# A block-causal attention mask added by TensorE: each masking matmul moved behind its own score map and cut from 64 contraction rows to one

## The reference, cut to what matters

```python
def attend(qb, qpb):
    s = jnp.einsum('bqhmd,bkhmd->bhmqk', qb, k).astype(jnp.float32) * scale
    mask = k_chunk[None, :] <= (qpb // CHUNK)[:, None]
    s = jnp.where(mask[None, None, None], s, -jnp.inf)
    p = jax.nn.softmax(s, axis=-1)
    pd = p[:, :, 0] - lam * p[:, :, 1]
    return jnp.einsum('bhqk,bkhv->bqhv', pd.astype(v.dtype), v)
```

## Time and profile before

| | us |
|---|---|
| median of 3 runs | 755.13 |
| lowest, highest | 754.0, 755.38 |
| the profiled execution | 755.38 |
| its span in the profile | 753.6 |
| PE (TensorE matmul) busy | 680.4 (90%) |
| DVE busy | 521.6 (69%) |
| ACT busy | 423.2 (56%) |
| mean granted TensorE clock | 0.959 |

### The profile page before, as it was taken

How to read it: one execution, slowest core, us unless ns; L and a number is a source line. 1 busy time by engine, 2 the same in 40 slices (tenths; PEclk the granted TensorE clock), 3 DMA queues, 4 the chain that set the end, 5 groups by cost and what they waited for, 6 DMA issues and landing times.

```text
span 753.6 us, 9418 instructions
## 1 busy us (share of the span) xinstructions
PE 680.4 (90%) x3464; PEld 548.7 (73%) x3464; DVE 521.6 (69%) x695; ACT 423.2 (56%) x600; POOL 139.3 (18%) x161
## 2 busy tenths in 40 slices
PE   5999999998879998889999389999999999999960
PEld 4898887776657666678888278888888888888850
DVE  4436745566566674466466868899999999988943
ACT  6645642345544443443333348778888877888750
POOL 4102930010000110100001302222222122222232
PEclk9999999999998999999999579999999999999976
DMA  8634143222580000230084869999999999999562
GB/s 312 200 114 157 54 160 142 65 82 107 204 339 10 2 1 1 62 134 1 1 310 168 337 243 352 368 381 374 381 373 379 376 375 385 374 382 374 187 239 76
DMA packets 33012, 161.63 MB, mean 214 GB/s; under 512 B 6238, under 2 KB 6572, under 8 KB 18253
## 3 DMA queue, kind: packets, MB, share of 16 engines
q1 hardware_dynamic: 23392, 140.39, 48.8%
q0 software_dynamic: 5488, 10.66, 5.2%
q10 hardware_dynamic: 4092, 10.08, 3.6%
HBM read 149.59 MB, written 20.55 MB: 226 GB/s over the span
## 4 chain that ended last, share of the span: by engine, by line
PE 70%; DVE 14%; DMA 7%; ACT 3%; issue 3%; POOL 1%; SPq 1%; POOLq 0%; ACTq 0%; DVEq 0%
PE pj L2098 40%; PE scores L2098 12%; PE tr_v L2098 10%; DVE wl L1407 3%; PE tr_a L2106 2%; PE scores L2475 2%; PE tr_v L2106 2%; DMA acc_rows<-y,idx_sb 1%; PE tr_a L2498 1%; DVE w_lo L1436 1%; DMA xT_raw<-in_xT 1%; DVE tiny L1658 1%; DVE w_lo L1407 1%; ACT prob L1127 1%; DVE hid L1407 1%
## 5 line engine op out<-in xcount | busy, mean ns | idle before, releaser
L1407 DVE TENSOR_TENSOR wl<-moe_raw,wh 128x2048 fp32r<-128x2048 f32 x96 | 218.5, 2290 | 32.0 <-ACT wh L899 31.5
L899 ACT ACTIVATE wh<-moe_raw 128x2048 fp32r<-128x2048 f32 x96 | 182.3, 1919 | 37.4 <-PE scores L2098 12.3
L2098 PE MATMUL pj<-w_hi,xT_hi 128*128 128x512 f32 (+2 forms) x192 | 70.7, 368 | 9.0 <-DVE w_lo L1436 8.3
L739 POOL TENSOR_SCALAR rs<-stat 128x1 f32<-128x1 f32 (+4 forms) x31 | 8.0, 258 | 339.4 <-ACT sq_scr L911 178.7
L2098 PE MATMUL pj<-w_hi,xT_lo 128*128 128x512 f32 (+2 forms) x192 | 68.9, 359 | 0.0
L2098 PE MATMUL pj<-w_lo,xT_hi 128*128 128x512 f32 (+2 forms) x192 | 68.9, 359 | 0.0
L794 POOL DMA_INDIRECT acc_rows<-y,idx_sb x14 | 22.2, 1589 | 207.0 <-ACT y L1329 193.0
L2098 PE MATMUL pj<-wh,xgh 128*128 128x512 f32 x128 | 52.5, 410 | 1.4 <-DVE xgl L1407 1.4
L2098 PE MATMUL scores<-wh,hTh 128*128 128x512 f32 x128 | 51.0, 398 | 1.4 <-DVE hTl L1407 1.4
L1436 DVE SCALAR_TENSOR_TENSOR w_lo<-raw,pack_a,w_hi 128x512 fp32r<-128x512 f32 (+2 forms) x64 | 43.8, 745 | 11.5 <-ACT w_hi L943 11.4
L2098 PE MATMUL tr_v<-wh,xgh 128*128 128x512 f32 x128 | 51.2, 400 | 0.0
(11 more groups left out here) (409 smaller groups left out, 1490.1 us busy)
## 6 DMA issues: line engine op xcount, KB each, us to landing
moe_raw<-in_w_exp_gate SPq DMA_DIRECT2D x32, 1024.0 KB, 7.9
moe_raw<-in_w_exp_up SPq DMA_DIRECT2D x32, 1024.0 KB, 9.1
moe_raw<-in_w_exp_down SPq DMA_DIRECT2D x32, 1024.0 KB, 8.9
raw<-in_dense SPq DMA_DIRECT2D x16, 1024.0 KB, 6.0
raw<-in_dense SPq DMA_DIRECT2D x8, 256.0 KB, 6.2
x_rows<-in_x_prompt SPq DMA_DIRECT2D x4, 512.0 KB, 11.2
xw<-in_x_prompt ACTq DMA_DIRECT2D x1, 2048.0 KB, 8.3
h_rows<-h ACTq DMA_DIRECT2D x4, 512.0 KB, 3.8
```

What stands on the lines that cost most here:

```text
L739: link(pool.tensor_scalar(rs[rows, n, cs], stat[rows, n, cs], EPS, None, ALU.add))
L899: act.activation(wh[s4][:, :], moe_raw[n % RING][:, :], ACT.Copy).then_inc(hi_done, 1)
L1407: return dve.tensor_tensor(out, a, b, op)
L2098: return pe.matmul(out, lhsT, rhs, start=start, stop=stop, skip_group_check=True)
```

## The change

The constants shrink to 65 partitions, with ones on all of them in the first 64 columns of `hide_q`. The mask of a map now takes a single partition of them, 0 for map 0 and 64 for map 1, so that it contracts over one row: 1 x -1e30. And it is issued right behind its own map's scores, ahead of the other map's. The increment of `sc_full` stays on the last mask.

```diff
-        hide_q = put("hide_q", [P, P], BF16)
-        hide_k = put("hide_k", [P, CH], BF16)
+        hide_q = put("hide_q", [CH + 1, P], BF16)
+        hide_k = put("hide_k", [CH + 1, CH], BF16)
...
             link(pool.memset(hide_q[:, :], 0.0))
-            for m in range(2):
-                link(pool.memset(hide_q[DH * m:DH * m + 1, 0:CH], 1.0))
+            link(pool.memset(hide_q[:, 0:CH], 1.0))
             ready(pool.memset(hide_k[:, :], -1e30))
...
                         out = half(key)[:, 512 * m:512 * m + 512]
                         mm(out[:, 0:nk], q, kT[ms, h, 0:nk], True, False)
+
+                        ins = mm(out[:, nk - CH:nk], hide_q[DH * m:DH * m + 1, :], hide_k[DH * m:DH * m + 1, :], False, True)
+                        if m == 1:
+                            ins.then_inc(sc_full, 1)
...
-                if t < 4:
-                    for m in range(2):
-                        ms = slice(DH * m, DH * m + DH)
-                        ins = mm(half(key)[:, 512 * m + nk - CH:512 * m + nk], hide_q[ms, :], hide_k[ms, :], False, True)
-                    ins.then_inc(sc_full, 1)
```

## The result

| | before | changed |
|---|---|---|
| median of 6 runs, us | 755.25 | 761.19 |
| lowest to highest, us | 754.0 to 757.65 | 759.26 to 762.98 |
| ratio, 95% interval | | 1.0085 (1.0061 to 1.0108) |
| the profiled execution, us | 755.38 | 764.52 |
| its span, us | 753.6 | 762.8 |

The change makes the kernel slower, by 0.85% in the ratio; the medians lie 5.9 us apart (0.8%). 759.6 was forecast, with a range of 757.0 to 763.5. The profiled execution of the changed kernel is 3.3 us above its median, so the trace is read for where its time goes, and the size is taken from the timed runs.

The account below looks back on a forecast made before the run. TensorE was taken to wait often for ACT or DVE until 240 us, then to bound through the scores. Steps grow 16.6 us, of which 4.4 reach the end: 755.38 + 4.4 = 759.8, stated as 759.6 us, range 757.0 to 763.5.

Parts of the forecast that it names:

- Rival 2: Masks on TensorE: one row is handled as 64 are, so the maps still overlap; 755.2 us, chance 0.10.
- The price of a change of shape: TensorE, where matmul row counts change: 0.13 us each, three more changes a step, 0.39 us.
- Steps 0 to 2 and 4 to 8: Tiles 0 to 2: growth mostly hidden under TensorE's waits for DVE and pdT; 0.1 us left at step 1.
- step 3: Last step of tile 0: DVE had waited 2.37 us for these scores, so what follows comes 0.72 later.
- The whole walk: Lateness followed step by step through attention, from step 0 to step 16: 4.5 us late at its end.
- the nine steps that count: Attention steps whose growth reaches the end; 0.2 us more in each step makes 1.9 us.
- rival 1: Around 223.7 us: the clock falls all the same, 7.2 us more in sum, 762.5 us; chance 0.23.
- step 10: Tile 2: TensorE at +0.3 takes a 0.97 wait, bound by DVE's xw at -0.6; 0.1 if the clock falls.
- The clock: From 223.7 to 230.5 us: stays at 2.4 GHz instead of 1.2, TensorE work some 2.7 us shorter.
- steps 7 and 8: Before 224.47 us: their growth, 0.93 + 1.14, is hidden in waits; they fill 2.1 us of idle time.
- The limit: DVE at diff_sq, 232.64 us: it had waited 1.46 us and is next, so not all 2.7 us is gained.
- Rival 3: Steps 1 to 9: idle time swallows the series, both half-clock stretches come back; 756.0 us, chance 0.05.

Follow-up runs that it names:

- 32 rows: Changed kernel with masks over 32 rows instead of one, against the kernel before: 761.32 us against 757.61, ratio 1.0059.
- 33 rows: Changed kernel with masks over 33 rows instead of one, against the kernel before: 758.40 us against 757.61, ratio 0.9991.
- tiles 0 and 1 alone: Kernel before with the change (one row, behind its own map) for tiles 0 and 1 only: 756.35 us against 755.63, ratio 1.0000.
- the fill at step 6: Eight unused fp32 matmuls behind step 6's product with the values: in the kernel before 753.69 us, in the changed one 758.97, each against 755.63.
- three such fills elsewhere: Kernel before with fills before step 0's product, step 18's output projection and the last transposes of the mixed rows: 752.12 us against 756.45, ratio 0.9933.

## Why the prediction was right, and where it was not

- *What bounds the kernel, and that the two maps run side by side and won't any more:* right. It rested on one line, two passes begun within 20 ns, and it is most of the effect: map 1 behind map 0 makes up 10.4 of the 15.2 us of TensorE time added, the changes of shape the rest. Rival 2 (the mask keeps the scores' shape) was wrong for 1 and 32 rows, and describes 33 rows exactly.
- *The price of a change of shape, 0.13:* this is the term that was mis-sized. From the mask to the next map it is 0.13 (206.29 to 206.42), the mask's own time included, but before a mask only 0.10. All three together come to 0.30 a step, where 0.39 was booked. The growth of a step was forecast as 0.93 at t=1 and 1.35 at t=3; it is 1.38 - 0.54 = 0.84 and 2.23 - 0.96 = 1.27. Over 16 steps that is 15.2 us of TensorE time instead of 16.6.
- *What reaches the end:* right where it can be read. Steps 0 to 2 and 4 to 8 mostly hidden, step 3 paid through DVE; tiles 0 and 1 alone cost 0.9 us of 5.9 added. From step 12 to 16, 3.9 of 5.1 are paid. The whole walk gave 4.4 us with the clock kept and 7.2 with it fallen; steps 0 to 16 took 4.0 more with 32 rows and 7.0 more in the changed kernel. The agreement is in part luck: with the measured price the nine steps that count add 0.8 less, and the same walk would give some 3.6 and 6.4. (The walk itself ends at 4.5 and is taken as 4.4, and rival 1's sum has 0.2 for step 10 where its sentence has 0.1; neither matters.)
- *The clock:* this is the step that was half wrong. "I take it that the clock stays at 2.4 GHz there" failed in the changed kernel's profile, which is rival 1, and held in the run with 32 rows. What the profile shows in its place is 1.2 GHz from 225.7 to 232.4, with TensorE busy 2.70 of the 3.4 us before; the reason given for the forecast, that steps 7 and 8 fill the idle time, does not decide it. The timed median, 5.9 us more, lies between the two sums, so the number does not tell them apart. The kernel alone doesn't decide it, since the clock differs between runs of the same work; what does decide it is open, but in all three profiles with the fill at step 6 it stayed up. The limit, that DVE is next in line 1.46 us earlier, was right.
- *Rival 3, not slower:* never near, since its premise, that a change of shape costs nothing, was false, and both stretches of half clock, at 189.5 and at 223.7, would have had to go; the changed kernel has them at 191.5 and 225.7.
- *The median:* 759.6 forecast, 761.2 measured. The 1.6 us between them are likely the clock of those runs in which it falls, less the 0.09 per step by which the price was too high; no run shows this, since only one execution of the changed kernel has a profile. How often it falls is not known.

## What to carry to other kernels

When two matmuls with short contractions run side by side on different partitions, whatever is issued between them must lie on their side of the border in rows (here 33 rows went with 64, and 32 and 1 did not); look for lines with x4 where the program has two by two, and for starts a few ns apart. Less work in an instruction (1 row for 64) is no gain if it takes it away from the row shape that its neighbours share. And a loss on TensorE is to be read wait by wait: the same edit cost nothing that the timing shows at tiles 0 and 1 and in the profile three quarters of its length at tile 3.

## What the runs showed of the hardware that I had not expected

- The halves of the array seem to run ahead of the program's order. With map 0, mask 0, map 1, mask 1 issued in this order at equal shape, map 1 still ran beside map 0 (0.54 us for all four passes), and the masks came last together. The profile doesn't name the map of a pass, nor the order in which the instructions reached TensorE; the reading rests on the changed kernel, where the two passes of one map start 0.32 us apart, while here the first two start within 10 ns.
- The border between 32 and 33 rows is sharp: 1.39 us for a step at t=1 with 32 rows, 0.54 with 33.
- The clock fell after 3.4 us in which TensorE had been busy 2.70, much of it with scores and masks one after the other, and stayed up in the run with 32 rows over the same work and the same wait of 1.41 us. 1.7 us of extra fp32 matmuls without a use made the kernel before 0.34% faster, three such fills elsewhere 0.67%.
